# Sparse attention of the first mixer: top-k rounds placed apart, a zero-filled value expansion evacuated whole, and two half output products taken out of the merge

## The reference, cut to what matters

```python
score = jnp.einsum('bths,bth->bts', jax.nn.relu(dots), wi)       # index scores, causal
_, idx = lax.top_k(score, top_k)                                 # top_k = 128 keys of each query
logits = jnp.einsum('bthd,btkd->bthk', qa, kg) * (HEAD_DIM ** -0.5)
p = jax.nn.softmax(logits, axis=-1)
o_lat = jnp.einsum('bthk,btkc->bthc', p, vg)                     # values: 128 latent numbers per head
o = jnp.einsum('bthc,hcd->bthd', o_lat, w_uv)                    # expansion: 128 latent -> 64 per head
...
y_b = stick_breaking_attention(...)
merged = jax.nn.sigmoid(gate_a) * (y_a @ w_o_a[l]) + jax.nn.sigmoid(gate_b) * (y_b @ w_o_b[l])
x = x + merged @ w_out[l]
```

## Time and profile before

| what | us |
| --- | --- |
| median of three runs | 2051.87 (2051.33 to 2052.62) |
| the profiled execution's own time | 2053.45 |
| its span | 2051.4 |
| PE busy | 1894.2 (92%) |
| DVE busy | 962.3 (47%) |
| ACT busy | 687.4 (34%) |
| first mixer, sparse attention stretch | about 684 to 772 of the span |

### The profile page before, as it was taken

The page is one execution under the profiler, slowest core; times in us unless marked ns, Lnnn a source line. Parts: engine busy times, 40 slices in busy tenths (PEclk is TensorE's granted clock), DMA queues, the critical chain, the costliest instruction groups (busy, mean ns, idle before and its releaser), DMA issues.

```text
span 2051.4 us, 21550 instructions
## 1 busy us (share of the span) xinstructions
PE 1894.2 (92%) x8662; PEld 1364.3 (67%) x8662; DVE 962.3 (47%) x1529; ACT 687.4 (34%) x1119; POOL 87.8 (4%) x121
## 2 busy tenths in 40 slices
PE   8999999898989889999999999999999977888887
PEld 6888888775778767888888888876784333333332
DVE  5433544368667886544344457656771111111113
ACT  5321322345555364332222234665641110010110
POOL 0000000100000001000000000000001111111100
PEclk9999999998999999999999999999999999999999
DMA  6433332344333304333233233221189999999997
GB/s 199 144 98 104 101 93 83 63 78 56 76 68 62 98 21 144 93 93 102 82 108 98 83 103 94 71 57 47 40 320 393 405 404 406 409 411 411 410 412 307
DMA packets 262154, 351.21 MB, mean 171 GB/s; under 512 B 11872, under 2 KB 225888, under 8 KB 237472
## 3 DMA queue, kind: packets, MB, share of 16 engines
q1 hardware_dynamic: 252432, 326.42, 47.7%
q0 software_dynamic: 9616, 23.34, 3.3%
HBM read 337.19 MB, written 20.45 MB: 174 GB/s over the span
## 4 chain that ended last, share of the span: by engine, by line
PE 65%; DMA 17%; DVE 10%; ACT 5%; issue 1%; SPq 1%; DVEq 0%; POOLq 0%; ACTq 0%
PE bank L183 64%; DMA large<-w_up 14%; SPq L225 1%; DMA stage<-w_in 1%; PE bank L186 1%; ACT T L189 1%; ACT wH L189 1%; DMA large<-pair_results 1%; ACT p L189 1%; DVE PTL L195 1%; DVE score L219 1%; DVE y L195 1%; DVE top L216 1%; DVE p L198 1%; DVE score L201 0%
## 5 line engine op out<-in xcount | busy, mean ns | idle before, releaser
L183 PE MATMUL bank<-hH,wH 128*128 128x512 f32 x1104 | 438.3, 397 | 18.9 <-DVE stage0L L195 9.9
L183 PE MATMUL bank<-hL,wH 128*128 128x512 f32 x1104 | 431.7, 391 | 0.0
L183 PE MATMUL bank<-large,xF 128*64 128x512 f32 x1024 | 243.5, 618 | 72.6 <-DMA large<-w_up 63.1
L189 ACT ACTIVATE wH<-stage 128x1024 fp32r<-128x1024 f32 (+3 forms) x231 | 227.9, 997 | 110.0 <-PE bank L183 83.9
L183 PEld LDWEIGHTS bank<-hH,wH 128*128 128x128 f32 x1104 | 209.0, 189 | 65.5 <-DVE stage0L L195 9.8
L183 PEld LDWEIGHTS bank<-hL,wH 128*128 128x128 f32 x1104 | 209.0, 189 | 44.2 <-issue 1.9
L183 PEld LDWEIGHTS bank<-large,xF 128*64 128x64 f32 x1024 | 82.2, 141 | 209.0 <-issue 161.8
L183 PE MATMUL bank<-hidH,wH 128*128 128x512 f32 x352 | 138.7, 394 | 2.0 <-DVE stage2L L195 0.8
L183 PE MATMUL bank<-hidL,wH 128*128 128x512 f32 x352 | 137.3, 390 | 0.0
L183 PE MATMUL bank<-large,hF 128*64 128x512 f32 x512 | 119.7, 610 | 2.6 <-DVE hF L195 2.6
L195 DVE TENSOR_TENSOR xF<-bank,gain 128x512 f32<-128x512 f32 x30 | 20.8, 692 | 157.1 <-PE bank L186 157.1
(11 more groups left out here) (502 smaller groups left out, 3267.4 us busy)
## 6 DMA issues: line engine op xcount, KB each, us to landing
large<-w_gate SPq DMA_DIRECT2D x64, 1024.0 KB, 29.1
large<-w_up SPq DMA_DIRECT2D x64, 1024.0 KB, 28.8
large<-w_down SPq DMA_DIRECT2D x64, 1024.0 KB, 29.2
stage<-w_in SPq DMA_DIRECT2D x58, 512.0 KB, 4.2
stage<-w_gate SPq DMA_DIRECT2D x44, 512.0 KB, 3.9
stage<-w_up SPq DMA_DIRECT2D x44, 512.0 KB, 3.8
stage<-w_down SPq DMA_DIRECT2D x16, 512.0 KB, 4.2
pair_results<-zero POOLq DMA_DIRECT2D x8, 512.0 KB, 3.0
```

What stands on the lines that cost most here:

```text
L183: return self.e.matmul(*a, **k) if self.e is not None else Nothing()
L189: return self.e.activation(*a, **k) if self.e is not None else Nothing()
```

## The change

Five edits, all in the first mixer.

1. The seven `topk` rounds (all of block 3) that stood among logits(1) to expand(0) now stand one by one from logits(4) to expand(3). `values(0)` moves ahead of one gate's evacuation, `expand(0)` behind logits(5).
2. `logits`: DVE waits for both exponentials and inverts both sums in one RECIPROCAL of 128x2, then scales both heads.
3. The expansion weights of two heads are stored with 64 zero columns between them (192 columns instead of 128). For each head pair the head's 64 columns and the zeros form a 128-column stationary tile, and the two heads of a pair accumulate into the same 128 columns of one bank. PE issues 12 matmuls of 128 columns for a group instead of 6 of 256; ACT and DVE take the group out in one operation of 128x2x128 each. The weights' split becomes two operations on ACT and four on DVE, and three memsets write the zeros once (`zero_wuv`).
4. `out_b(0)` stands between values(7) and expand(7), `out_b(1)` behind expand(7): they are the y_b halves of merges 0 and 1, with those merges' weights. Merges 0 and 1 keep the y_a half only.
5. With these steps the weight preparation of the units 2 and 3 moves to the `out_b` steps (merges 0 and 1 then ask for three units ahead).

```diff
+            wuvH, low01 = sb([128, 4, 192], F32R, "wuvH"), sb([128, 2, 192], F32R, "wuvL")
+            low23 = nc.alloc_sbuf_tensor_at("wuvL23", [128, 2, 192], F32R, offset=top_end)
...
+            def out_weights(m):
+                return unit([(0, wcols("w_o_a", m * 128, 128, 0, 4)), (512, wcols("w_o_b", m * 128, 128, 0, 4))], 8, 128, ("mm", "ob" if m >= 2 else "oa", m))
+
+            def out_b(m):
+                s = Step("out_b", m=m, unit=out_weights(m), bank=banks.take(("gb", m)))
+                outs[m] = s.unit, s.bank
+                add(s)
...
             logits(1)
-            topk(1)
             gate()
...
             turn_p(2)
             logits(4)
+            values(0)
             evict()
-            values(0)
-            topk(2)
-            expand(0)
             topk(1)
...
             expand(6)
             values(7)
+            out_b(0)
             expand(7)
+            out_b(1)
...
                     elif s.kind == "expand":
                         pe.wait_ge(*after("ol", n))
+                        free(s.bank)
                         for c2 in range(2):
-                            free(s.banks[c2])
-                            mm3(s.banks[c2].t[:, 0:256], both(M.wuv, slice(None), 2 * s.g + c2, slice(None)),
-                                both(M.ol, slice(None), slice(256 * c2, 256 * c2 + 256)), True, True).then_inc(*did("mm", "expand", n, c2))
+                            for e in range(2):
+                                at = 256 * c2 + 128 * e
+                                t = mm3(s.bank.t[:, 128 * c2:128 * c2 + 128], [part[2 * s.g + c2][:, 64 * e:64 * e + 128] for part in M.wuv],
+                                        both(M.ol, slice(None), slice(at, at + 128)), e == 0, e == 1, skip=True)
+                        t.then_inc(*did("mm", "expand", n))
...
+                    elif s.kind == "out_b":
+                        pe.wait_ge(*after("w_lo", s.unit.i))
+                        pe.wait_ge(*after("yb", 7))
+                        free(s.bank)
+                        for k in range(4):
+                            t = mm3(s.bank.t[:, :], (s.unit.H[:, 4 + k, :], s.unit.L[:, 4 + k, :]), (M.yb[0][:, k, :], M.yb[1][:, k, :]), k == 0, k == 3)
+                        t.then_inc(*did("mm", "ob", m))
...
                         t.then_inc(*did("mm", "oa", m))
+                        if m < 2:
+                            continue
...
-                        weights_for(s.u)
+                        weights_to(s.u.i + (3 if m < 2 else AHEAD))
...
+                        dve.wait_ge(*after("pexp", n + 1))
+                        dve.reciprocal(M.st[:, n:n + 2, 1:2], M.st[:, n:n + 2, 1:2]).then_inc(*did("pinv", n))
+                        dve.wait_ge(*after("pinv", n))
                         for e in range(2):
-                            dve.wait_ge(*after("pexp", n + e))
-                            dve.reciprocal(M.st[:, n + e, 1:2], M.st[:, n + e, 1:2]).then_inc(*did("pinv", n + e))
-                            dve.wait_ge(*after("pinv", n + e))
                             dve.tensor_scalar(s.p[e].t[:, 0:W], s.p[e].t[:, 0:W], M.st[:, n + e, 1:2], None, ALU.mult).then_inc(*did("prob", n + e))
...
-                        for c2 in range(2):
-                            for e2 in range(2):
-                                pp, at = slice(64 * e2, 64 * e2 + 64), slice(i * 128, (i + 1) * 128)
-                                dve.wait_ge(*after("yah", n, c2, e2))
-                                low(M.ya[1][pp, 2 * s.g + c2, at], s.banks[c2].t[pp, 128 * e2:128 * e2 + 128], M.ya[0][pp, 2 * s.g + c2, at]).then_inc(*did("ya", n, c2, e2))
+                        blocks, at = slice(2 * s.g, 2 * s.g + 2), slice(i * 128, (i + 1) * 128)
+                        dve.wait_ge(*after("yah", n))
+                        low(M.ya[1][:, blocks, at], s.bank.t[:, 0:256].rearrange("p (a n) -> p a n", a=2), M.ya[0][:, blocks, at]).then_inc(*did("ya", n))
```

More of the change, by code:

```diff
@@ L450, in mixer1 @@
             assert place[0] == mark1
-            M.va, M.wuv = pair([128, 4, 128], "va"), pair([128, 4, 128], "wuv")
+            M.va = pair([128, 4, 128], "va")
+            wuvH, low01 = sb([128, 4, 192], F32R, "wuvH"), sb([128, 2, 192], F32R, "wuvL")
+            low23 = nc.alloc_sbuf_tensor_at("wuvL23", [128, 2, 192], F32R, offset=top_end)
+            M.wuv = [wuvH[:, a, :] for a in range(4)], [t[:, a, :] for t in (low01, low23) for a in range(2)]
+            M.wuv_parts = [(wuvH, slice(0, 4)), (low01, slice(0, 2)), (low23, slice(2, 4))]
             M.amask, M.widx = sb([128, 1280], F32R, "amask"), sb([128, 4, 8], F32, "widx")
@@ L596, in expand @@
                 i, g, _ = jobs[4 * grp]
-                add(Step("expand", n=grp, i=i, g=g, banks=[banks.take(("ya", grp, c2, 1)) for c2 in range(2)]))
+                add(Step("expand", n=grp, i=i, g=g, bank=banks.take(("ya", grp))))
             add(Step("kb_zero", n=0))
+            outs = {}
+            def out_weights(m):
[4 more added lines that the diff above has]
+                add(s)
+            add(Step("zero_wuv"))
             vw_rows(0)
@@ L817, in mixer1 @@
             logits(5)
+            expand(0)
+            topk(1)
             turn_p(4)
@@ L869, in mixer1 @@
             for m in range(8):
-                s = Step("merge", m=m, u=unit([(0, wcols("w_o_a", m * 128, 128, 0, 4)), (512, wcols("w_o_b", m * 128, 128, 0, 4))], 8, 128, ("mm", "ob", m)))
-                s.ba, s.bb = banks.take(("ga", m)), banks.take(("gb", m))
+                s = Step("merge", m=m)
+                if m in outs:
+                    s.u, s.bb = outs[m]
+                    s.ba = banks.take(("ga", m))
+                else:
+                    s.u = out_weights(m)
+                    s.ba, s.bb = banks.take(("ga", m)), banks.take(("gb", m))
                 s.s1, s.s2, s.mt = loaded[2 * m], loaded[2 * m + 1], mt.take(("mg", m))
@@ L2049, in mixer1_stage @@
                             weights_for(g.unit)
-                    elif s.kind in ("dense", "rows"):
+                    elif s.kind in ("dense", "rows", "out_b"):
                         weights_for(s.unit)
@@ L2082, in mixer1_stage @@
                         act.wait_ge(*after("wuv_in",))
-                        act.activation(M.wuv[0][:, :, :], M.wuvF[:, :, :].rearrange("p (a b) d -> p a (b d)", b=2), ACT.Copy).then_inc(*did("hi_wuv"))
+                        act.wait_ge(*after("wuv_zero"))
+                        for e in range(2):
+                            act.activation(M.wuv_parts[0][0][:, :, 128 * e:128 * e + 64], M.wuvF[:, e::2, :], ACT.Copy).then_inc(*did("hi_wuv", e))
                     elif s.kind == "amask0":
@@ L2108, in mixer1_stage @@
                         if n:
[L2109 removed]
+                            act.wait_ge(*after("mm", "expand", n - 1))
                         act.activation(M.ol[0][:, :], s.bank.t[:, :], ACT.Copy).then_inc(*did("olh", n))
                     elif s.kind == "expand":
[L2112 to L2117 removed]
+                        act.wait_ge(*after("mm", "expand", n))
+                        act.activation(M.ya[0][:, 2 * s.g:2 * s.g + 2, i * 128:(i + 1) * 128], s.bank.t[:, 0:256].rearrange("p (a n) -> p a n", a=2),
+                                       ACT.Copy).then_inc(*did("yah", n))
                     elif s.kind == "split_qk":
@@ L2588, in mixer1_stage @@
                     elif s.kind == "split_wuv":
-                        dve.wait_ge(*after("hi_wuv",))
-                        low(M.wuv[1][:, :, :], M.wuvF[:, :, :].rearrange("p (a b) d -> p a (b d)", b=2), M.wuv[0][:, :, :]).then_inc(*did("wuv"))
+                        for e in range(2):
+                            dve.wait_ge(*after("hi_wuv", e))
+                            at = slice(128 * e, 128 * e + 64)
+                            for t, blocks in M.wuv_parts[1:]:
+                                x = low(t[:, :, at], M.wuvF[:, e::2, :][:, blocks, :], M.wuv_parts[0][0][:, blocks, at])
+                            x.then_inc(*did("wuv", e))
+                    elif s.kind == "zero_wuv":
+                        dve.wait_ge(*after("nx", "g_mix"))
+                        for t, _ in M.wuv_parts:
+                            x = dve.memset(t[:, :, 64:128].bitcast(F32), 0.0)
+                        x.then_inc(*did("wuv_zero"))
                     elif s.kind == "topk":
```

18 lines of the change are left out of this document (6 added, 12 removed).

## The result

| kernel | median us (range, runs) | ratio to before (95%) |
| --- | --- | --- |
| before | 2051.86 (2049.91 to 2056.12, 9) | 1 |
| the change | 2059.06 (2055.84 to 2062.35, 9) | 1.0029 (1.0018 to 1.0039) |

What follows compares the result with a forecast made beforehand. Limits: PE to 705, DVE to about 765, both to 771.70, then PE. Terms: +2.5 (rounds, reciprocal, expansion, PTH wait), +0.6 new wait, +0.6 expand(5), -2.6 merge, +0.6 weights = +1.7, giving 2053.6 us; range 2047.5 to 2059.

Steps and rivals of the forecast that it cites:

- rival B: Low PE clock behind the mask, after PE's idle ahead of logits(12): +4.8 to +8, 2056.7 to 2059.9 us; chance 0.17.
- Rounds: Seven top-k rounds behind logits(4): DVE starts it earlier, -1.6; rounds at 1.40 each cost 9.8 against 4.4, +5.4.
- Reciprocal: One merged reciprocal per head pair lengthens each pair on DVE by one scaling: +3.6 to PTL of pair 13.
- the term of -4.7: Five expansions before PTL of pair 13, each taken out by DVE in 0.33 instead of 1.27: 0.94 saved each.
- PE's +0.6 per expansion: Twelve 128-column matmuls take 1.33 against 0.70 for six of 256; hidden while DVE is the limit.
- New wait and low clock: PE idles 5.7 ahead of logits(12) for the mask; a low clock then makes DVE wait at PTL(10): +0.6, ends 0 and 2.2.
- B's first price: Low clock behind the mask makes DVE wait 2.2 instead of 0.6 at PTL(10).
- the +4.7 forecast: From DVE's maxima of logits(4) to its PTL of pair 13: 5.4 + 3.6 - 4.7 - 0.2 + 0.6.
- Merge: End of the stretch, values(7) to the merges: out_b parts fill PE's idles, 1.33 stays for 3.93, -2.6.
- Rival C: The first merges become DVE's, or out_b delays expand(7): the -2.6 goes, 2056.2 us; chance 0.10.
- Rival A: DVE's savings count whole, merged reciprocal free, 128-column matmuls at half price, no low clock: 2046.9 to 2048.2 us; chance 0.18.
- the term of +0.6: Early split of the expansion weights: four subtracts of 1.27 for one of 0.68 less 0.09, +0.6, between 0 and 0.7.

Runs made afterwards that it cites:

- e7: The kernel before with only the change's order of top-k rounds, gates and values(0): median 2058.52 us, ratio 1.0042 (1.0028 to 1.0055).
- e9: e5 with two of the three top-k rounds behind logits(4) put earlier: median 2047.21 us, ratio to before 0.9975.
- e6: The kernel before with only the reciprocal merged over the two heads of a pair: median 2055.35 us, ratio 1.0025 (1.0016 to 1.0034).
- e2: The change with top-k rounds, values(0) and expand(0) back in the old order: median 2055.16 us, ratio to before 1.0012 (1.0002 to 1.0022).
- e3: The kernel before with the new expansion and the two output parts, old order and reciprocals: median 2049.52 us, ratio 0.9984 (0.9975 to 0.9994).
- e1: The change with the two reciprocals of a pair apart again: median 2057.70 us, ratio to before 1.0027 (1.0015 to 1.0040).
- e4: The kernel before with the new expansion alone: median 2053.79 us, ratio 1.0012 (1.0002 to 1.0022).
- e10: e9 with the new expansion as well: median 2046.02 us, ratio to before 0.9975 (0.9964 to 0.9985).
- e5: The kernel before with only out_b(0) and out_b(1) put at the mixer's end: median 2049.14 us, ratio 0.9982 (0.9973 to 0.9991).
- e11: The change with the gate's eviction back ahead of values(0): median 2056.26 us, ratio to before 1.0024 (1.0015 to 1.0033).
- e8: e3 with 16 products that nobody reads put between values(0) and expand(0): median 2048.85 us, ratio to before 0.9982.
- e12: e10 with out_b(0) moved between values(0) and expand(0): median 2041.82 us, ratio to before 0.9949 (0.9935 to 0.9962).

## Why the prediction came out as it did

The direction and several terms were right, the size was not: +1.7 for 5.9 (3.7 to 8.0). That the time is that of rival B is in part luck, as said below.

**Rounds: the step "without them DVE can start at 704.9: -1.6" failed.** I looked at what DVE did ahead of logits(4) and not at what stood in its order just in front: PTL of turn_p(2), which needs the one PT buffer that values(0) reads. The start stayed at 22.4 us behind ybL, in the change and in e7, and DVE waits 4.52 instead. The other half, 1.40 for each round behind the start, is borne out: e9, with two of them taken away, gained 2.5, and e7, with +5.4 of rounds and +1.2 of DVE's other waits, lost 7.2.

**Reciprocal: right by itself.** +3.6 forecast, +3.2 measured alone (e6, by the ratio 5.1, 3.3 to 7.0). With the new expansion in the old order it is 2.7 up to olL(5) (e2 against e3). In the change it comes to 1.8 (against e1): the waits at the reciprocal grow as forecast, but DVE's waits at other places, 3.9 in e1, are 2.3 in the change, so part of what comes late would have waited anyway.

**Expansion: the term of -4.7 was mis-sized.** Its price on DVE is what I said, 0.42 for 1.27. But I let every saved 0.94 count, because DVE works 11.2 of 12.5 us. It brings 0.8 up to olL(5) with the old order (e4), 2.4 with the new one (e1 against e7) and 2.5 with early rounds (e10 against e9). The rest comes back as DVE's waits for ACT and PE: from the maxima of logits(4) to PTL of pair 13 its waits other than at the reciprocal are 0.2 in e5 and 3.7 in e3, 0.7 in e9 and 2.8 in e10, 1.4 in e7 and 3.9 in e1. -4.7 and these differences make -1.2, -2.6 and -2.2. I had PE's +0.6 per expansion hidden under DVE, and reckoned it at the full clock; in the low clock behind the idle it is +1.3, PE becomes the limit there, and in e2, e3 and e4 the low clock itself lasts 20.5 us for the 13.6 of before. The Trainium skill's 55.6 ns between matmuls of 128 columns (TensorE: Matmul & The Clock Gate, "Wait — 56ns, not 53.3ns?") is not what these take: 0.112 at the full clock, 0.214 at the lower level; the row of 136 columns had told the first.

**New wait and low clock: the place right, the size between forecast and B.** 5.10 ahead of logits(12), clock 0.72 in 745 to 757; PTL(10) waited 0.86 and one pair's maxima 0.2: 1.1 for the 0.6 in the sum. B's first price was 2.2. But I had the low clock ahead of the mask gone with the wait of 4.13: in its place stood 4.16 ahead of logits(5), for the eviction, and the clock of 709.5 to 722 is 0.59. There DVE waits 0.83 at yaL and 0.40 at PTL, 1.2 in all. The Trainium skill's rule that an idle TensorE returns to half rate (the same page, "Why this matters for your kernels") agrees with this trace at all three long waits, of 4.16, 2.79 and 5.10 us. B, which rests on it, was closest to the time, but not by its own prices: values(6) to values(7), its larger part, ran at the full clock, and PTL(10) waited 0.86 and not 2.2. That wait for the eviction I had not foreseen; e11 took only 0.6 us of it away, and its share stays open.

**Sum for the slow part.** From the maxima of logits(4) to PTL of pair 13 DVE's waits other than at its reciprocal are 0.2 before and 2.3 in the change, +2.1; the sum had +0.6 and -0.2. The 1.7 between them, on the +4.7 forecast, makes 6.4, against 6.7 in the table. So in the change's own order of time rounds, reciprocal and expansion have the sizes that the forecast gave them on DVE, and what was left out are its waits for the others. With the start that did not come, the whole is 1.7 + 1.6 + 2.0 + 0.2 - 0.1 for the four rows of the table, and -0.4 for the weights: 5.0. The ratio says 5.9 (3.7 to 8.0).

**Merge: right.** -2.6 forecast, -2.7 in the change, -3.3 alone. Rival C falls: no idle from values(7) to the third merge.

**Rival A falls with e4 and e6.** The new expansion alone makes the kernel no faster, and the merged reciprocal is not free.

**Weights: the term of +0.6 was too large.** The four subtracts of wuvL take 0.81 from their start to the next operation's, for 0.60 before, and not 1.27. DVE's kaL, which ends that chain, comes at the same distance from the work ahead of it as before within 0.2.

**The parts do not add up.** Alone they give +7.2, +3.2, +0.1 and -3.3 in the stretch, together 7.2, and the change has 4.8; up to olL(5) it is 7.2 + 3.2 - 0.8 = 9.6 for 6.7. The expansion and the reciprocal change sides with the order: where DVE has more work (new order) the one saves more, and where it waits more the other seems to cost less. By the ratios the sum would be 12.5 for 5.9, with intervals of 4 to 6 us each. The four kernels with expansion and parts say the same: up to olL(5) e3 has -0.8, with the merged reciprocal +1.9 (e2), with the new order +4.9 (e1), with both +6.7 (the change). By the ratios to before they are -3.3, +2.5, +5.5 and +5.9: there the reciprocal seems to cost 5.7 in the old order and 0.4 in the new. The profiles of e1 and e2 hold low clocks behind olL(5) that those of e3 and the change lack, and lose some 3 us each there. That goes the same way, but one profile of each does not settle it. What is left open: why the clock falls near the end of the stretch in some profiles with the new expansion, and with it whether e4 is slower than before or level.

## What to carry to other kernels

Before work is taken off an engine ahead of a start, find the instruction that stands just in front of the start in its order and ask what that one waits for: if it waits for something else, the engine only idles, and the work was free where it stood. A saving on the busiest engine counts only up to the next engine's load, and that load is to be reckoned at the clock that the rows show there, not at the full one. An idle of some us on TensorE is a place for products that must be done anyway: here 2.8 us of them, moved to such a place, were worth 4.2 by the medians (of the 4.8 in the profiles, 1.6 is a low clock near the end that comes and goes), while products that nobody reads, put there in e8, gained nothing clear.

## What the runs showed of the hardware

- Matmuls of 128 columns with other weights each start 0.112 apart at the full clock (770.62 to 771.74 in the change) and 0.214 at the lower level (719.23 to 721.37 in e4). Those of 256 columns of the kernel before start 0.118 apart (769.57 to 770.04) and 0.213 (710.22 to 711.07): half the columns take nearly the same time. What both kinds share is one weight load each; that it sets the pace is not shown.
- Idles of 2.31 us in e8 and of 2.79 in the change were accompanied by a low clock as one of 4.13 was before; it began within 0.8 us of the idle's end. One of 1.65 in the kernel before brought none. One of 1.41 was followed by one in e10, and by none in the change.
- The low clock behind the idle of 4.12 or 4.13 ahead of expand(0) lasted 13.6 us before and in e5, 20.5 in e3 and e4, 10.2 in e10 and 6.8 in e9: with the same idle ahead its length differs by kernel (one profile of each).
- The executions of one program spread over 3.7 us (e8) to 10.5 us (e2). In the profiles here the last ybL lies between 682.0 and 686.6; a low clock at other places goes with part of it (0.89 and 0.97 in 500 to 560 us in the change and before), and e1 and e12 differ by 2.3 there at the same clocks.
